# The way out of an RWKV layer: values centred before the recurrence, group norm with tokens on the partitions, the output product one half of the tokens at a time, and experts chosen on the logits

## The chip, the cores and the metric

The kernel runs on one core of a Trainium2 chip. The metric is the device time of one execution in microseconds (us), the median of three. The core's engines run side by side, each through its own list of instructions in order, and wait for each other on semaphores: TensorE (PE), VectorE (DVE), ScalarE (ACT), GpSimd (POOL), and SyncE (SP), which here only issues DMAs. Matrix products land in PSUM, 8 banks of 512 fp32 columns on 128 partitions; everything else lives in SBUF.

## The reference

The kernel computes two decoder layers on 256 tokens of width 1024, with 16 learned tokens ahead. Only the end of the second layer's RWKV part and the start of its experts matter here. Cut to that:

```python
def step(S, inp):                        # per head of 64: matrix state S
    sa = einsum('bhvk,bhk->bhv', S, a_t)
    S = S * w_t + sa[..., None] * b_t + v_t[..., None] * k_t
    return S, einsum('bhvk,bhk->bhv', S, r_t)
_, out = lax.scan(step, S0, xs)
mu  = mean(out, axis=-1)                 # over the 64 values of a head
var = mean(square(out - mu), axis=-1)
out = (out - mu) * rsqrt(var + GN_EPS) * gn_w + gn_b
y = (out + bonus).reshape(B, T, D)
h = h + (y * g) @ w_o
u = rmsnorm(h, ffn_norm)
probs = softmax(u @ w_router)            # 8 experts, top 2, their share renormalised
```

## The kernel before

Each engine's program is written out by hand in the order in which it runs; a `wait_ge(semaphore, n)` holds the engine until another has counted that far. Nothing is scheduled automatically, so an engine's order is the order of the code.

**The recurrence** is done in 5 chunks of 64 positions (`NCH`, the index `c`; the first holds padding and the learned tokens). Tensors stand with channels on the partitions: 8 pairs of heads (`PAIRS`), a pair's two heads on partitions 0 to 63 and 64 to 127 (`HROWS`). First a triangular system is solved for all chunks at once (`level_y` L1045, `level_x` L1060; ACT takes each result out of PSUM at L1581). Then the loop over chunks: right-hand side (L1079, L1082; evicted by ACT L1591), solution U (L1089; evicted by DVE L2068), state update (L1100, L1102; DVE L2073, L2080) and, from chunk 1 on, the outputs (L1112, L1114, L1116; evicted by ACT L1595 into `w_a`, channels on the partitions). The state and the outputs are linear in the values `v_a`, which are turned per chunk and head by a product with a 64x64 unit matrix (`turned`, kind "TV").

**The exit.** After the last chunk PE turns the residual `hT` into token order (L1125, 16 transposes), sums each head's outputs with `headones` (L1130), DVE subtracts the mean (L2089), ACT squares (L1604), PE sums the squares (L1136), ACT takes the root (L1607), and DVE does four operations on each of 8 pairs: reciprocal, gain, bias plus bonus, gate (L2092 to L2099). The output product (L1146) contracts over channels: 8 steps, each for both halves of the tokens (`t`) and both halves of the columns (`n`), so that all four results end together. DVE adds the residual (L2105), ACT squares and roots (L1611, L1613), DVE normalises (L2113), PE turns the normalised tokens (L1158), ACT copies them (L1621) and PE makes the logits (L1166, 16 products of 8 columns). DVE then softmaxes and picks two experts in 20-odd small steps (L2131 to L2150), PE ranks the tokens (L1172 to L1176), and the tokens of the first two experts are gathered (L1190).

**The experts** come last: 8 experts, every one over all its weights, streamed by SP into a ring of 7 tiles of 1 MB, split by ACT and DVE into two fp32r parts (L1640, L2179) and multiplied at L1237 to L1239. Ahead of the logits, ACT and DVE already split the first two tiles (L1617, L2118). SP starts to load this ring when the last outputs are evicted (L488, L485). POOL makes the low half of the normalised tokens (L618) from ACT's high half (L1624).

## Time and profile before

| | us |
|---|---|
| median of three runs | 1696.16 (1696.04 to 1699.24) |
| the profiled execution, its own time | 1698.43 |
| its span, from first to last instruction | 1696.7 |
| PE busy | 1643.3 (97%) |
| DVE busy | 1263.2 (74%) |
| ACT busy | 985.2 (58%) |
| POOL busy | 86.1 (5%) |

The busy share alone says that PE works nearly always. Where it does not, and what it does at the exit of the recurrence, is seen in the views by time. All times in this document that have the form of a place (at 644.5) are microseconds from the start of the span.

### The profile page before, as it was taken

To read this page: it belongs to the slowest core of one execution; us is meant where nothing else is said; L and a number is where in the kernel's file an instruction comes from. 1 tells how busy PE (TensorE), PEld (TensorE's weight loads), DVE (VectorE), ACT (ScalarE), POOL (GpSimd) and SP (SyncE) were. 2 spreads that over 40 slices of the span, in tenths; PEclk is the share of its full clock that TensorE was granted. 3 is DMA by queue.
4 is the path that set the end of the run, shared out by engine and by line. 5 is a ranking of instruction groups with operands and counts; after the bars stand their busy time and mean duration, and the time that the engine had idled before them with its cause. 6 is when DMAs were issued, how large, how long until landed. Compare 5 with 4: busy or idle time off the path is not lost.

```text
span 1696.7 us, 27438 instructions
## 1 busy us (share of the span) xinstructions
PE 1643.3 (97%) x11321; PEld 1405.2 (83%) x11321; DVE 1263.2 (74%) x1202; ACT 985.2 (58%) x1003; POOL 86.1 (5%) x134
## 2 busy tenths in 40 slices
PE   7999999998999999699999999999999999999997
PEld 5879999997778996588888888888888888888885
DVE  4655555534486746598888898988988988898986
ACT  5655443331423222577667776767767777767674
POOL 3462000001000000100000000000000000000000
PEclk9989999999999999799999999999999999999999
DMA  7115555542440005199999999999999999999993
GB/s 276 51 51 186 179 176 178 176 150 58 148 144 6 3 4 187 64 358 380 378 356 343 366 364 372 374 341 357 372 354 384 364 349 353 369 361 381 363 373 148
DMA packets 191312, 432.66 MB, mean 255 GB/s; under 512 B 10003, under 2 KB 11027, under 8 KB 191188
## 3 DMA queue, kind: packets, MB, share of 16 engines
q1 hardware_dynamic: 191148, 430.82, 70.8%
q8 instruction: 91, 1.49, 0.4%
q14 instruction: 33, 0.27, 0.0%
q10 hardware_dynamic: 40, 0.08, 0.0%
HBM read 429.82 MB, written 1.05 MB: 254 GB/s over the span
## 4 chain that ended last, share of the span: by engine, by line
PE 90%; DVE 5%; ACT 3%; issue 1%; DMA 0%; ACTq 0%; DVEq 0%
PE ps L1237 18%; PE ps L1239 18%; PE ps L1238 18%; PE ps L682 6%; PE ps L684 6%; PE ps L683 6%; PE ps L926 3%; PE ps L1146 2%; PE ps L1261 1%; PE ps L1060 1%; PE ps L1045 1%; PE ps L1190 1%; PE ps L1004 1%; DVE arena L1984 1%; PE ps L1016 1%
## 5 line engine op out<-in xcount | busy, mean ns | idle before, releaser
L2179 DVE TENSOR_TENSOR wsplit<-raw_w,wsplit 128x2048 fp32r<-128x2048 f32 x336 | 751.4, 2287 | 78.4 <-ACT wsplit L1640 78.4
L1640 ACT ACTIVATE wsplit<-raw_w 128x2048 fp32r<-128x2048 f32 x336 | 624.9, 1918 | 59.4 <-PE ps L1239 59.4
L1237 PE MATMUL ps<-wsplit,xsplit 128*128 128x512 f32 x896 | 354.4, 396 | 0.0
L1239 PE MATMUL ps<-wsplit,xsplit 128*128 128x512 f32 x896 | 349.7, 390 | 0.0
L1238 PE MATMUL ps<-wsplit,xsplit 128*128 128x512 f32 x896 | 349.1, 390 | 0.0
L1239 PEld LDWEIGHTS ps<-wsplit,xsplit 128*128 128x128 f32 x896 | 168.2, 188 | 35.8
L1237 PEld LDWEIGHTS ps<-wsplit,xsplit 128*128 128x128 f32 x896 | 168.3, 188 | 33.4 <-DVE wsplit L2179 0.5
L1238 PEld LDWEIGHTS ps<-wsplit,xsplit 128*128 128x128 f32 x896 | 168.6, 188 | 33.1
L1237 PE MATMUL ps<-wsplit,hsplit 128*128 128x512 f32 x448 | 175.3, 391 | 1.5 <-DVE hsplit L2209 1.5
L1238 PE MATMUL ps<-wsplit,hsplit 128*128 128x512 f32 x448 | 174.5, 390 | 0.0
L1239 PE MATMUL ps<-wsplit,hsplit 128*128 128x512 f32 x448 | 174.5, 389 | 0.0
L1677 ACT ACTIVATE arena<-ps 128x512 f32<-128x512 f32 x56 | 33.5, 598 | 178.6 <-PE ps L1239 178.6
L1886 DVE TENSOR_TENSOR ffn_lo<-ffn_raw,ffn_hi 128x2048 fp32r<-128x2048 f32 x42 | 95.0, 2293 | 53.4 <-ACT ffn_hi L1480 53.2
L684 PE MATMUL ps<-u_hi,ffn_lo 128*128 128x272 f32 x448 | 129.0, 288 | 0.0
L683 PE MATMUL ps<-u_lo,ffn_hi 128*128 128x272 f32 x448 | 128.9, 288 | 0.0
L682 PE MATMUL ps<-u_hi,ffn_hi 128*128 128x272 f32 x448 | 128.9, 288 | 0.0
L1480 ACT ACTIVATE ffn_hi<-ffn_raw 128x2048 fp32r<-128x2048 f32 x42 | 78.6, 1903 | 37.8 <-PE ps L684 37.8
L1237 PEld LDWEIGHTS ps<-wsplit,hsplit 128*128 128x128 f32 x448 | 84.2, 188 | 18.7 <-DVE wsplit L2179 1.7
L926 PE MATMUL ps<-arena 128*128 128x272 f32 x384 | 93.8, 403 | 5.6 <-DVE arena L1938 5.1
L1239 PEld LDWEIGHTS ps<-wsplit,hsplit 128*128 128x128 f32 x448 | 84.1, 188 | 17.7
L1238 PEld LDWEIGHTS ps<-wsplit,hsplit 128*128 128x128 f32 x448 | 84.2, 188 | 16.9
L926 PEld LDWEIGHTS ps<-arena 128*128 128x128 f32 x384 | 73.5, 194 | 24.4 <-issue 6.4
(395 smaller groups left out, 2324.1 us busy)
## 6 DMA issues: line engine op xcount, KB each, us to landing
raw_w<-in_moe_w_gate SPq DMA_DIRECT2D x114, 1024.0 KB, 7.1
raw_w<-in_moe_w_up SPq DMA_DIRECT2D x112, 1024.0 KB, 7.8
raw_w<-in_moe_w_down SPq DMA_DIRECT2D x112, 1024.0 KB, 7.1
ffn_raw<-in_ffn_w_up SPq DMA_DIRECT2D x14, 1024.0 KB, 5.1
ffn_raw<-in_ffn_w_gate SPq DMA_DIRECT2D x14, 1024.0 KB, 5.2
ffn_raw<-in_ffn_w_down SPq DMA_DIRECT2D x14, 1024.0 KB, 5.1
ffn_raw<-in_attn_w_qkv SPq DMA_DIRECT2D x6, 1024.0 KB, 10.8
ffn_raw<-in_attn_w_o SPq DMA_DIRECT2D x4, 1024.0 KB, 11.0
```

The lines of the kernel that those rows point to most:

```text
L682: mm(o, w_hi_, x_hi_, start=first, stop=False)
L683: mm(o, w_hi_, x_lo_, start=False, stop=False)
L684: return mm(o, w_lo_, x_hi_, start=False, stop=last_)
L926: last = mm(ps[:, j % 4, 0:T], slot_k[s][:, k, (m % 4) * P:(m % 4 + 1) * P], xm[which // 2][:, k, :], start=(k == 0), stop=(k == KC - 1))
L1146: last = mm(ps[:, 2 * t + n, :], w_a[:, k, CH + t * P:CH + (t + 1) * P], slot_k[n][:, k, :], start=(k == 0), stop=(k == KC - 1))
L1237: mm(o, x_[0], w_[0], start=first_, stop=False)
L1238: mm(o, x_[0], w_[1], start=False, stop=False)
L1239: return mm(o, x_[1], w_[0], start=False, stop=last_)
L1480: A(ffn_hi[:, m % NFH, :], ffn_raw[:, ffn_at(m), :], ACT.Copy).then_inc(hi_ok, 1)
L1640: A(wsplit[:, m % NRING, 0, :], raw_w[:, m % NRAW, :], ACT.Copy).then_inc(w_hi, 1)
L1886: v.tensor_tensor(ffn_lo[:, ffn_at(m), :], ffn_raw[:, ffn_at(m), :], ffn_hi[:, m % NFH, :].bitcast(F32), ALU.subtract).then_inc(lo_ok, 1)
L2179: v.tensor_tensor(wsplit[:, m % NRING, 1, :], raw_w[:, m % NRAW, :], wsplit[:, m % NRING, 0, :].bitcast(F32), ALU.subtract).then_inc(w_lo, 1)
```

## The change

**Centring.** The matrix that turns the values is no longer the unit matrix but the unit matrix less 1/64, `wide`, built by POOL. The values, and with them state and outputs, come out less their mean over the head; the mean is never computed from the outputs.

**Outputs by tokens.** The two operands of the output products change places, so that tokens stand on the partitions: chunks 1 and 2 are the first 128 tokens, 3 and 4 the second. A pair's two heads write the same 64 partitions of two banks, 6 and 7, where before each wrote its own 64 partitions of one bank. The outputs stay in PSUM. ACT squares them there (`gn_squares`), DVE sums over each head (`gn_sums`), ACT takes the root of 16 numbers per token (`gn_root`), DVE scales (`gn_scaled`), PE turns them back (`y_turned`), and DVE gates them (`gated`) with two prepared tensors. For the first half all this stands inside the loop, in chunks 2 to 4.

**Prepared tensors.** POOL makes (bonus + bias) * gate and gate * gain ahead, behind `bonus_ok`. The residual is turned into token order much earlier, ahead of the projections, and copied by ACT into `htok`.

**The output product** runs one quarter after the other (`out2(t, n, ...)`). What stands in between: the turning of the second half of the outputs, of the finished tokens (not yet normalised, `tokens_turned`), and the first three quarters of the logits. The gain of the norm is multiplied into the router's weights, and the token's own scale into the logits.

**The choice** works on the logits: softmax is taken out of the way, and the exponentials are used only for the shares of the two chosen.

**Tables.** ACT gets a dummy Sqrt ahead of the loop over chunks and a dummy Exp ahead of the split of the tokens, so that the function tables are loaded there.

```diff
@@ POOL: the centring matrix, behind the masks; the prepared tensors @@
+            fill(wide[:, :], -1.0 / HD)
+            one(g.affine_select(out=wide[:, :], in_=wide[:, :], pattern=[[-1, P]], compare_op=ALU.not_equal, fill=1.0 - 1.0 / HD,
+                                base=0, channel_multiplier=1), masks_ok)
...
-            pool.wait_ge(utT_mm, 4)
+            pool.wait_ge(bonus_ok, 1)
+            pool.wait_ge(l2_ev, 3 * KC)
+            for m in range(PAIRS):
+                last = g.tensor_scalar(bonus[:, m, :], bonus[:, m, :], par[:, m, R_GNB:R_GNB + 1], None, ALU.add)
+            one(last)
+            one(g.tensor_tensor(bonus[:, :, :], bonus[:, :, :], g_a[:, :, :], ALU.mult))
+            for m in range(PAIRS):
+                last = g.tensor_scalar(g_a[:, m, :], g_a[:, m, :], par[:, m, R_GNW:R_GNW + 1], None, ALU.mult)
+            own.done(last, gb_ok)
@@ PE: the residual turned ahead of the projections; the values @@
+            for t in range(2):
+                for half in range(2):
+                    for q in range(4):
+                        k = 4 * half + q
+                        last = tr(ps[:, 4 + 2 * t + half, q * P:(q + 1) * P], hT[:, k, META + t * P:META + (t + 1) * P], ident[:, :])
+                    last.then_inc(ht_mm, 1)
...
-                        unit = mask64[rows, 8, :] if kind == "TV" else Dg[rows, c, p, :]
+                        unit = wide[rows, rows] if kind == "TV" else Dg[rows, c, p, :]
@@ PE: the loop over chunks @@
+            def y_turned(t):
+                pe.wait_ge(yn_ok, t + 1)
+                for h in range(2):
+                    for q in range(4):
+                        last = tr(ps[:, 4 + h, q * P:(q + 1) * P], yn[:, 4 * h + q, :, :].rearrange("p a d -> p (a d)"), ident[:, :])
+                    last.then_inc(yt_mm, 1)
...
+                if c == NCH - 1:
+                    y_turned(0)
                 if c:
+                    t, toks = (c - 1) // 2, HROWS[(c - 1) % 2]
                     for h in range(2):
                         pe.wait_ge(u_ev, c * 2 + h + 1)
-                        if c >= 2:
-                            pe.wait_ge(ot_ev, (c - 2) * 2 + h + 1)
+                        if t:
+                            pe.wait_ge(yn_ok, 1)
                         for p in range(4 * h, 4 * h + 4):
-                            o = [ps[rows, 6 + h, (p % 4) * CH:(p % 4 + 1) * CH] for rows in HROWS]
+                            o = [ps[toks, 6 + e, p * CH:(p + 1) * CH] for e in range(2)]
                             for e, rows in enumerate(HROWS):
-                                mm(o[e], S[(c - 1) % 2][rows, p, :], r_a[rows, p, cs_(c)], start=True, stop=False)
+                                mm(o[e], r_a[rows, p, cs_(c)], S[(c - 1) % 2][rows, p, :], start=True, stop=False)
...
@@ PE: behind the loop, in place of L1120 to L1168 @@
+            out2(0, 0, range(KC))
+            y_turned(1)
+            out2(0, 1, range(KC))
+            out2(1, 0, range(KC))
+            tokens_turned(0, 0)
+            tokens_turned(0, 1)
+            out2(1, 1, range(4))
+            logits(0, 0)
+            logits(0, 1)
+            tokens_turned(1, 0)
+            out2(1, 1, range(4, KC))
+            logits(1, 0)
+            tokens_turned(1, 1)
+            logits(1, 1).then_inc(lg_mm, 1)
@@ ACT @@
+            A(mstat[:, 1, 0:1], epsD, ACT.Sqrt)
             for c in range(NCH):
                 for h in range(2):
                     act.wait_ge(rhs_mm, c * 2 + h + 1)
                     A(RHS[:, 4 * h:4 * h + 4, :], quad(h), ACT.Copy).then_inc(rhs_ev, 1)
...
+                if c == 3:
+                    gn_root(0)
+                if c == 2 or c == 4:
+                    gn_squares(c // 2 - 1)
+            gn_root(1)
...
+            square_tokens(0)
             for m in range(AHEAD):
                 act.wait_ge(ring_in[m], ring_was[m] + 16)
                 A(wsplit[:, m, 0, :], raw_w[:, m, :], ACT.Copy).then_inc(w_hi, 1)
...
+            turned(0)
+            turned(1)
+            turned(2)
+            square_tokens(1)
+            A(mstat[:, 1, 0:1], epsD, ACT.Exp)
             for t in range(2):
+                act.wait_ge(utok_ok, 2 * t + 2)
                 A(utok_hi[:, t, :], utok[:, t, :], ACT.Copy).then_inc(utok_hi_ok, 1)
@@ DVE @@
+                if c == 3:
+                    gn_sums(0)
                 for h in range(2):
                     dve.wait_ge(u_mm, c * 2 + h + 1)
                     v.tensor_copy(U[:, 4 * h:4 * h + 4, :], quad(2 + h)).then_inc(u_ev, 1)
+                if c == 3:
+                    gn_scaled(0)
...
+            gated(0)
+            dve.wait_ge(ld_router, 16)
+            v.tensor_tensor(router[:, :, :], router[:, :, :], par[:, :, R_FFNN + 1:R_FFNN + 2].to_broadcast([P, KC, EXPERTS]), ALU.mult)
+            gn_sums(1)
+            gn_scaled(1)
...
             dve.wait_ge(lg_mm, 1)
-            step(v.tensor_copy(rt(3), ps[:, 0, 0:16].rearrange("p (t e) -> p t e", t=2)))
-            step(v.tensor_reduce(col(0), rt(3), AX, ALU.max))
-            step(v.tensor_tensor(rt(1), rt(3), wide(0), ALU.subtract), lg_sub)
-            dve.wait_ge(lg_exp, 1)
-            step(v.tensor_reduce(col(1), rt(2), AX, ALU.add))
-            step(v.reciprocal(col(2), col(1)))
-            step(v.tensor_tensor(rt(3), rt(2), wide(2), ALU.mult))
+            step(v.tensor_tensor(rt(3), ps[:, 0, 0:16].rearrange("p (t e) -> p t e", t=2), wide(7), ALU.mult))
+            step(v.tensor_reduce(col(3), rt(3), AX, ALU.max))
+            step(v.tensor_tensor(rt(1), rt(3), wide(3), ALU.subtract), lg_sub)
```

How instructions move is shown at three places. First PE from the last outputs of the last chunk on. Before (L1116 outputs, L1125 residual turned, L1130 and L1136 sums over heads, L1146 output product):

```order
L1116 MATMUL ps<-arena 64x64 x2
L1125 MATMUL ps<-ident,hT 128x128 [waits ot_ev]
L1125 MATMUL ps<-ident,hT 128x128 x15
L1130 MATMUL ps<-arena,headones 128x256 x4
L1130 MATMUL ps<-arena,headones 128x256 [waits gn_x] x4
L1136 MATMUL ps<-arena,headones 128x256 [waits gn_sqd,ht_cp]
L1136 MATMUL ps<-arena,headones 128x256 [waits gn_sqd] x3
L1136 MATMUL ps<-arena,headones 128x256 [waits gn_sd,gn_sqd] x4
L1146 MATMUL ps<-arena 128x512 [waits slot_in1,y_ok,slot_in0,gn_sd]
L1146 MATMUL ps<-arena 128x512 x3
```

The same place in the changed kernel (L1147 outputs, L1156 output product, L1097 outputs turned, L1167 tokens turned, L1173 logits):

```order
L1147 MATMUL ps<-arena 64x64 x2
L1156 MATMUL ps<-arena 128x512 [waits y_ok,slot_in1,slot_in0]
L1156 MATMUL ps<-arena 128x512 [waits y_ok] x7
L1097 MATMUL ps<-ident,arena 128x128 [waits yn_ok]
L1097 MATMUL ps<-ident,arena 128x128 x7
L1156 MATMUL ps<-arena 128x512 x8
L1156 MATMUL ps<-arena 128x512 [waits y_ok] x8
L1167 MATMUL ps<-ident,arena 128x128 [waits yn_ok,acc_ok]
L1167 MATMUL ps<-ident,arena 128x128 x3
L1167 MATMUL ps<-ident,arena 128x128 [waits yn_ok,acc_ok]
L1167 MATMUL ps<-ident,arena 128x128 x3
L1156 MATMUL ps<-arena 128x512 x4
```

The output product now stands right behind the outputs, and 8 + 8 transposes and part of the logits stand between its quarters. Second, ACT where the loop over chunks begins. Before (L1581 the triangular system, L1591 right-hand sides, L1595 outputs):

```order
L1581 ACTIVATE arena<-ps 128x512 [waits x_mm] x23
L1591 ACTIVATE arena<-ps 128x256 [waits rhs_mm] x4
L1595 ACTIVATE arena<-ps 128x4x64 [waits ot_mm] x2
L1591 ACTIVATE arena<-ps 128x256 [waits rhs_mm] x2
L1595 ACTIVATE arena<-ps 128x4x64 [waits ot_mm] x2
```

Now (L1628 the dummy Sqrt, L1632 right-hand sides, L1621 squares, L1626 the root):

```order
L1609 ACTIVATE arena<-ps 128x512 [waits x_mm] x23
L1628 ACT_TABLE_LOAD
L1628 ACTIVATE mstat<-normcol 128x1
L1632 ACTIVATE arena<-ps 128x256 [waits rhs_mm] x6
L1621 ACTIVATE arena<-ps 128x512 [waits ot_mm]
L1621 ACTIVATE arena<-ps 128x512
L1632 ACTIVATE arena<-ps 128x256 [waits rhs_mm] x2
L1626 ACTIVATE qstat<-qstat,normcol 128x16 [waits gn_ss]
```

A table load and the dummy stand between the last eviction of the system and the first right-hand side; the evictions of outputs are gone, and two squares stand ahead of chunk 3's right-hand sides. Third, DVE from the third residual sum to the first step of the choice. Before, all four residual sums stood together ahead of the norm (L2105) and the two splits (L2118) right ahead of the choice (L2131). Now (L2180 the splits, L2162 residual sums, L2185 a turned quarter copied, L2166 and L2170 the norm, L2198 and after it the choice):

```order
L2180 TENSOR_TENSOR wsplit<-raw_w,wsplit 128x2048 [waits w_hi] x2
L2162 TENSOR_TENSOR arena<-arena,ps 128x512 [waits wo2_mm] x2
L2185 COPY arena<-ps 128x4x128 [waits utT_mm]
L2166 RECIPROCAL rcol<-rcol 128x1 [waits n4_std]
L2170 SCALAR_TENSOR_TENSOR utok<-arena,rcol 128x512 [waits dve_own]
L2170 SCALAR_TENSOR_TENSOR utok<-arena,rcol 128x512
L2198 TENSOR_TENSOR route<-ps,rcol 128x2x8 [waits lg_mm]
L2199 TENSOR_REDUCE rcol<-route 128x2 [waits dve_own]
L2200 TENSOR_TENSOR route<-route,rcol 128x2x8 [waits dve_own]
```

The splits have moved ahead of the last two residual sums; from the first step of the choice to the mask that PE waits for there are now 14 steps on DVE, with no wait for ACT among them.

## Rows read from the trace of the kernel before

**Rows 1.** Windows: stretch, its length, busy time of the engines, granted clock, DMA share, GB/s

```profile
685.00:714.00 29.00, 16.25 (x91) 14.23 (x92) 17.09 (x42) 14.44 (x23) 4.65 (x2) 0.71 0.21 73
714.00:1000.00 286.00, 286.00 (x1310) 237.24 (x1309) 250.13 (x152) 210.12 (x155) 0.00 (x0) 1.00 0.98 357
```

**Rows 2.** What SP's queue waited for: total us, times, longest

```profile
SPq L485 <- DVE wsplit L2179: 842.8, 329, 24.8
```

**Rows 3.** The chain that ended last, in order of time: start, us, what

```profile
644.48 0.39 ACT arena L1595
644.92 1.97 PE ps L1125 x16
...
656.47 27.72 PE ps L1146 x64
...
684.21 0.70 DVE arena L2105
684.93 1.16 ACT utok L1611 x2
686.11 0.30 ACT rcol L1613
...
690.63 4.59 PE ps L1166 x32
...
701.24 0.59 PE ps L1172 x2
...
713.97 0.23 PE ps L1237
```

**Rows 4.** Timeline of ACT: start, us, instruction, idle time before it and its releaser

```profile
610.84 0.82 ACT L1591 ACTIVATE arena<-ps 128x256 f32<-128x256 f32 x2
...
630.86 0.38 ACT L1595 ACTIVATE arena<-ps 128x256 f32<-128x256 f32 x1 [1.02 <-PE ps L1116]
...
651.27 1.28 ACT L1607 ACT_TABLE_LOAD   x1
...
691.82 2.02 ACT L1624 ACTIVATE utok_hi<-utok 128x1024 fp32r<-128x1024 f32 x2
```

**Rows 5.** Timeline of PE, the outputs of chunk 3

```profile
635.59 0.28 PE L1112 MATMUL ps<-arena 64*64 64x64 f32 x4
635.71 0.28 PE L1114 MATMUL ps<-arena 64*64 64x64 f32 x4
```

**Rows 6.** Timeline of DVE in chunk 3 and in the choice of experts

```profile
633.89 0.42 DVE L2068 COPY arena<-ps 128x256 f32<-128x256 f32 x1 [0.27 <-PE ps L1089]
...
698.92 0.18 DVE L2140 TENSOR_TENSOR route<-route,rcol 128x16 f32<-128x16 f32 x1
...
701.00 0.18 DVE L2146 TENSOR_TENSOR route<-route 128x16 f32<-128x16 f32 x1
```

**Rows 7.** DVE by line and form: a sum over 256 columns

```profile
L1734 DVE TENSOR_REDUCE kstat<-rsq 128x4 f32<-128x256 f32 x2 | 0.8, 414 | 1.7 <-ACT rsq L1359 1.7
```

**Rows 8.** Timeline of PE in the attention of layer 0

```profile
85.00 0.73 PE L728 MATMUL ps<-kz,qT 64*128 64x272 f32 x4
85.56 0.41 PE L731 MATMUL ps<-kz,qT 64*128 64x144 f32 x4
```

**Rows 9.** Timelines of POOL and DVE side by side, early and at the choice

```profile
64.16 4.58 POOL L550 TENSOR_TENSOR ffn_lo<-ffn_raw,ffn_hi 128x2048 fp32r<-128x2048 f32 x1
...
78.00 3.14 POOL L559 TENSOR_SCALAR probs<-probs,stat 128x144 f32<-128x144 f32 x4 [5.78 <-DVE stat L1801]
...
693.07 4.65 POOL L618 TENSOR_TENSOR utok_lo<-utok,utok_hi 128x1024 fp32r<-128x1024 f32 x2 [276.64 <-ACT utok_hi L1624]
...
65.08 3.68 DVE L1799 TENSOR_TENSOR stat<-stat 128x4 f32<-128x4 f32 x1 [2.08 <-ACT stat L1406]
...
695.66 2.09 DVE L2133 TENSOR_TENSOR route<-route,rcol 128x16 f32<-128x16 f32 x1
```

**Rows 10.** Timeline of PE at the start of the projections

```profile
403.61 16.69 PE L926 MATMUL ps<-arena 128*128 128x272 f32 x55 [5.10 <-DVE arena L1938]
```

More of the change, by code:

```diff
@@ L1115, in _ @@
                             for e, rows in enumerate(HROWS):
-                                last = mm(o[e], v_a[rows, p, cs_(c)], both[c][1][rows, 0, p, :], start=False, stop=True)
+                                last = mm(o[e], both[c][1][rows, 0, p, :], v_a[rows, p, cs_(c)], start=False, stop=True)
+                    if c % 2 == 0:
                         last.then_inc(ot_mm, 1)
-            pe.wait_ge(ot_ev, 2 * (NCH - 1))
-            for t in range(2):
-                for half in range(2):
-                    for q in range(4):
-                        k = 4 * half + q
-                        last = tr(ps[:, 2 * t + half, q * P:(q + 1) * P], hT[:, k, META + t * P:META + (t + 1) * P], ident[:, :])
-                    last.then_inc(ht_mm, 1)
@@ L1139, in _, with out2, tokens_turned @@
-            pe.wait_ge(gn_sd, PAIRS)
+            def out2(t, n, ks):
+                for k in ks:
+                    if n == 0:
+                        pe.wait_ge(y_ok, 2 * t + k // 4 + 1)
+                    last = mm(ps[:, 2 * t + n, :], w_a[:, k, CH + t * P:CH + (t + 1) * P], slot_k[n][:, k, :],
+                              start=(k == 0), stop=(k == KC - 1))
+                    if k == KC - 1:
+                        last.then_inc(wo2_mm, 1)
+            def tokens_turned(t, half):
+                pe.wait_ge(acc_ok, 2 * t + half + 1)
+                if t == 0:
+                    pe.wait_ge(yn_ok, 2)
+                for q in range(4):
+                    k = 4 * half + q
+                    last = tr(ps[:, (6, 4)[t] + half, q * P:(q + 1) * P], acc[:, t, k * P:(k + 1) * P], ident[:, :])
+                last.then_inc(utT_mm, 1)
@@ L1509, in _ @@
             norm_std_(3)
+            act.wait_ge(norm_u, KC)
+            act.wait_ge(ht_mm, 4)
+            for n in range(4):
+                own.done(A(htok[:, n // 2, (n % 2) * BLK:(n % 2 + 1) * BLK], ps[:, 4 + n, :], ACT.Copy), ht_cp)
             def take(j):
@@ L1586, in quad, with gn_squares, gn_root @@
                 return ps[:, b, 0:4 * CH].rearrange("p (a b) -> p a b", a=4)
+            def gn_squares(t):
+                act.wait_ge(ot_mm, t + 1)
+                if t:
+                    act.wait_ge(gn_ss, t)
+                for e in range(2):
+                    last = A(gsq[:, e, :, :], ps[:, 6 + e, :].rearrange("p (a b) -> p a b", a=PAIRS), ACT.Square)
+                own.done(last, gn_sqd)
+            def gn_root(t):
+                act.wait_ge(gn_ss, t + 1)
+                own.done(A(qstat[:, 1, t, :], qstat[:, 0, t, :], ACT.Sqrt, bias=eps_gn, scale=1.0 / HD), gn_sd)
+            A(mstat[:, 1, 0:1], epsD, ACT.Sqrt)
             for c in range(NCH):
@@ L1613, in _, with turned @@
                 own.done(A(rcol[:, 6, t:t + 1], normcol[:, 2, t:t + 1], ACT.Sqrt, bias=epsD, scale=1.0 / D), n4_std)
+            def turned(n):
+                t, half = n // 2, n % 2
+                act.wait_ge(utT_mm, n + 1)
+                own.done(A(utT[:, 4 * half:4 * half + 4, t * P:(t + 1) * P],
+                           ps[:, (6, 4)[t] + half, :].rearrange("p (a b) -> p a b", a=4), ACT.Copy), utT_cp)
+            square_tokens(0)
             for m in range(AHEAD):
@@ L2119, in _ @@
                     .then_inc(w_lo, 1)
+            added(2)
+            added(3)
+            dve.wait_ge(utT_mm, 4)
+            own.done(v.tensor_copy(utT[:, 4:8, P:2 * P], ps[:, 5, :].rearrange("p (a b) -> p a b", a=4)), utT_dve)
+            normed(1)
             col = lambda n: rcol[:, n, :]
```

157 lines of the change are left out of this document (62 added, 95 removed).

## The prediction, made before the changed kernel was run

> **What bounds the kernel now.** I read the windows first. From 714 to 1000 PE is busy in all of 286.00 us [rows 1], and so on to the end of the experts, at the full granted clock. The weights come at 357 GB/s and the DMA share is 0.98, which could make the stream the bound; but SP's queue spent 842.8 us, in 329 waits, on DVE's freeing of a ring tile [rows 2]: it waits for buffers, not they for it. So the experts last as long as PE needs, whenever they start, and what counts is when the first expert product (L1237) starts: at 713.97 [rows 3]. In the window 685 to 714 PE is busy in 16.25 of 29.00 us at a mean clock of 0.71 [rows 1].
>
> The chain in order of time then gives the exit piece by piece [rows 3]. The last outputs are evicted from 644.48. The output product starts at 656.47: 12.0 us for residual, sums over heads and norm. It takes 27.72 us for 64 records, two for each of the 32 products, so 0.87 us for each. The last residual sum is at 684.21, the logits start at 690.63, and PE's ranks wait until 701.24. From the end of the product to the ranks it is 17.0 us, and from the ranks to L1237 12.7 us, which the change leaves alone.
>
> **The change part by part.** Terms are shifts of L1237, plus is later.
>
> *Ahead of the loop over chunks.* The dummy Sqrt makes a table load of 1.28 us, which stood at 651.27 in the exit, stand ahead of ACT's first right-hand sides at 610.84 [rows 4]. PE has nothing to do there but the solution that needs them, and the whole loop is a chain behind it. With 0.3 for the dummy itself: **+1.6**. The Trainium skill (ScalarE: Activation LUTs, What ACT_TABLE_LOAD costs) puts a switch of sets at about 2.66 us, the load and a drain as long again. The trace has the load at 1.28 us and the next operation of ACT right behind it. By the page the term would be +2.9.
>
> *In the loop.* The output products keep count and shape; a pair's products follow each other every 0.12 us [rows 5], 24 pairs a chunk in four chunks. They now share the 64 output columns of the array and lie on different rows of it. The trace has that form in attention: L728 is two products of 64 rows on the same 128 output partitions, two banks, 272 columns, in 4 records. One such record takes 0.23 us (0.433 for 512 columns [rows 3], by 272/512). Four in a row would be 0.92; L731 starts 0.56 behind L728 [rows 8]. So they overlap; I take 0, bounds 0 and +11.2 (96 pairs at 0.117).
>
> Group norm of the first half: ACT squares from 630.86, where it evicted outputs before [rows 4], two PSUM operations, about 1.1; chunk 3's right-hand sides are queued behind them on ACT, wanted at 631.8 and so late by 0.1 with as much cover. DVE sums 1024 columns: 0.41 for 256 [rows 7] with about 0.17 of fixed cost (a step on 16 columns takes 0.18 [rows 6]) makes 1.2, done at 633.2, just when U can be copied. ACT's root hides behind the copies, the second of which is at 633.89 to 634.3 [rows 6]; reciprocal and two scalings (0.7 and 0.6, by the 0.70 of L2105 [rows 3]) end at 635.95. PE wants banks 6 and 7 for chunk 3 at 635.59 [rows 5] and now waits for that, with the outputs and all of chunk 4 queued behind: **+0.4**. The state update behind the scalings is late by 1.2, with 2 us of cover while the outputs run. If the squares came an operation later, this wait would grow one for one.
>
> The turn of the first half in chunk 4 is 8 of the 16 transposes that took 1.97 [rows 3]: **+1.0**. DVE's gating of it (4 operations of 0.7) ends before the last outputs do.
>
> *Behind the loop.* The product starts right behind the outputs instead of 12.0 us after 644.48: **-12.0**. Its 27.7 us stay. In between stand 8 transposes for the second half, 12 for finished tokens and 8 of 16 logit products: 20 x 0.123 + 8 x 0.287 (4.59 for 16 [rows 3]) = 2.5 + 2.3: **+4.8**. The waits in between are covered: the second half's norm needs about 4.5 us behind the last outputs, the first quarter gives 6.9; its gating is done within 4 us under the second quarter; DVE's two weight splits, 4.5 us, lie under the third.
>
> *From the end of the product to the ranks*, 17.0 before. Now: residual sum 0.15 + 0.7, square and root 1.5 (684.93 to 686.41 [rows 3]) with 0.1 ahead, so the root at +2.5. DVE normalises till +4.2; the last logits, on PE, are ready at +3.9. Then 14 steps to the mask, 0.208 apart (ten intervals from 698.92 to 701.00 [rows 6]), 2.9: the mask at +7.1, if nothing holds DVE. But ACT behind its root loads Exp (1.3, dummy 0.2) and copies the first half of the tokens (1.0, half of 2.02 [rows 4]); so POOL starts on the low half at about +5.2, when DVE stands at its sixth or seventh step, and works 2 x 2.33 us. A DVE operation on two SBUF operands doesn't run beside a two-operand one of POOL: one on 4 columns took 3.68 us and ended with POOL's from 64.16 to 68.74, and in the choice itself one took 2.09 us, till POOL ended at 697.72 [rows 9]. Most of the 14 steps are of that kind. So they end with POOL at +9.9, and six or seven more steps, 1.4, make +11.3: **-5.7**. Half of what removing steps saves is given back there.
>
> *At no cost.* The 16 early transposes stand in a gap of PE: it idles 5.10 us until 403.61 [rows 10]; at 0.123 they need 2.0, at half clock 4.0. ACT's four copies fall into its own gap there. If they ran over, the projections would start that much later. POOL's preparation starts at about 538 and needs, at 0.79 for each of 16 (3.14 for 4 [rows 9]) and 4.6 for the product, some 18 to 20 us; it is wanted at 642. It can hold DVE's two-operand steps in the grouping (up to 4.6 once); PE there runs eight banks ahead, over 6 us, so 0, bounds 0 and +4.6. The ring starts to fill some 3 us later, and the first tile is wanted 16 us after that.
>
> Sum: 1.6 + 0.4 + 1.0 - 12.0 + 4.8 - 5.7 = -9.9. The profiled execution is 1698.43 with a span of 1696.7, 2.3 above the median of 1696.16; the shift is the same for both. 1698.4 - 9.9 = 1688.5 for a profiled one, and **1686.3** as the median.
>
> **The rivals.**
> *The array doesn't overlap two products that share output columns.* Then each of 96 pairs costs 0.117 more, +11.2; and if the start-up seen in attention (0.56 against 0.46 for two records) is paid by every pair, another 0.1 each, +9.6. 1686.3 + 11.2 to + 20.8 is 1697.5 to 1707: slower. It decides from 0.10 us a pair. For it: no row has this form with 64 columns on 64. Against it: the attention products, as worked out above [rows 8]. The Trainium skill (TensorEngine Tiling (Array Packing), Gotcha 1: PSUM Pressure) says that different row tiles can't access one bank at the same time and go to different ones; banks 6 and 7 keep to that, so by the page too they overlap.
>
> *POOL doesn't hold DVE in the choice* (its start falls later, or DVE slips through). The mask is then at +7.1: -9.9 for that term, and 1682.1. For it: only a few tenths between the seventh step and POOL's start. Against it: DVE would need to finish seven more steps in that time.
>
> *The moved work delays the loop*: norm in chunk 3 late by one or two operations, POOL's preparation felt by PE, +2 to +5, so 1688 to 1691. For it: the chain squares, sums, root, reciprocal, scalings crosses engines five times, and I have 0.4 of its end uncovered.
>
> *The gain doesn't reach the end* since the stream sets the pace of the experts: the ring would be full either way at the start, so the time is before's plus what the ring fills later, 1696 to 1699. Against it: PE has no gap there, and the queue waits for buffers [rows 1, 2].
>
> **How the numbers follow.** Forecast 0.64; POOL doesn't hold 0.12; the loop delayed 0.14; gain lost in the stream 0.04; no overlap 0.06. The range must leave out no more than 2 in 10: from 1681.5 (POOL doesn't hold) to 1691.2 (the far end of loop delayed). 0.2% of this time, 3.4 us, is about what a measurement of this kernel can tell from no change; the border is at 1692.8. Faster: the first three, less a little of the delayed one for worse than I bound it, 0.88. Same: the stream and the mild end of no overlap, 0.07. Slower: the rest, 0.05.
>
> **What the profile of the changed kernel would show.** A table load between the last L1609 and the first L1632 of ACT, and the first solution (L1117) 1.6 us later behind the system than now. The outputs' pairs still 0.12 apart. A wait of PE for DVE's scalings ahead of chunk 3's outputs, below a microsecond. The output product right behind the outputs, and no wait of over 0.5 us until the logits are done. One or two DVE steps of over a microsecond in the choice, beside POOL. L1237's successor starting at about 704, and the experts as long as now (983 us from there to the span's end). The prediction is wrong if the pairs lie 0.23 apart, if PE waits for norm or gating between the quarters, or if the experts are longer.

## The result, and the profile after

The changed kernel took 1684.63 us (median; 1682.65 to 1686.13) against 1697.32 for the kernel before, measured beside it: a ratio of 0.9925, 95% interval 0.9913 to 0.9936. Two later measurements of the same pair gave 0.9949 (0.9935 to 0.9962) and 0.9919 (0.9905 to 0.9932), so 12.7, 8.5 and 13.5 us less. The mean of the three ratios, 0.9931, times 1696.16 is 1684.5; 1686.3 was predicted.

The chain that ended last, in order of time, of the changed kernel (start, us, what) stands against [rows 3]:

```profile
645.90 7.06 PE ps L1156 x16
652.97 0.87 PE ps L1097 x8
653.84 13.73 PE ps L1156 x32
667.57 0.88 PE ps L1167 x8
668.45 3.43 PE ps L1156 x8
671.88 1.69 PE ps L1173 x16
673.57 0.49 PE ps L1167 x4
674.06 3.45 PE ps L1156 x8
677.53 0.70 DVE arena L2162
678.25 1.16 ACT utok L1641 x2
...
682.53 2.13 DVE route L2207
684.68 2.27 DVE route L2209
...
688.25 0.60 PE ps L1196 x2
...
693.94 6.15 PE ps L1214 x24
...
701.66 0.23 PE ps L1261
```

The four quarters of the output product (L1156) follow each other, with turns and logits between them and no wait. They take 27.67 us together, as the product did before (27.72). Then comes the choice, with two steps above 2 us, and the first expert product (L1261) at 701.66 instead of 713.97 [rows 3]. One wait of PE stands outside this chain, ahead of the last quarter of the logits. The timeline of PE has it:

```profile
679.72 1.06 PE L1173 MATMUL ps<-router,arena 128*128 128x8 f32 x8 [0.78 <-DVE arena L2185]
```

The front of the kernel, nearly the same in both, doesn't take the same time in each execution. A timeline of ScalarE shows where the front ends, at the last result of the triangular system (L1609, before L1581). Changed kernel:

```profile
609.38 0.60 ACT L1609 ACTIVATE arena<-ps 128x512 f32<-128x512 f32 x1 [0.34 <-PE ps L1080]
609.99 1.28 ACT L1628 ACT_TABLE_LOAD   x1
611.29 0.20 ACT L1628 ACTIVATE mstat<-normcol 128x1 f32<-128x1 f32 x1
611.40 0.64 ACT L1632 ACTIVATE arena<-ps 128x256 f32<-128x256 f32 x2
```

and the kernel before:

```profile
610.35 0.60 ACT L1581 ACTIVATE arena<-ps 128x512 f32<-128x512 f32 x1 [0.34 <-PE ps L1060]
```

In the profiles of this study that place lies anywhere from 605.84 to 612.00. So below, kernels are compared by the **stretch** from there to the first expert product in the timeline of PE: 713.81 - 610.35 = 103.46 before, 701.49 - 609.38 = 92.11 after. From that product to the span's end it is 982.9 us in both. The gain of the change is thus 11.35 us in the first profile of the changed kernel, and 11.6 and 11.5 in its two repeats, each against the one profile of the kernel before.

### The profile page after: what moved, and what is told of

It is laid out like the page before. It is cut to its first block, busy times and chain, and to the rows that moved or that the text cites. A ratio compares the mean times of both kernels' runs of the same rounds, so it can differ in the third digit from the quotient of the medians.

```text
span 1684.4 us, 27376 instructions
## 1 busy us (share of the span) xinstructions
PE 1631.8 (97%) x11305; PEld 1396.5 (83%) x11305; DVE 1250.3 (74%) x1176; ACT 977.8 (58%) x986; POOL 107.9 (6%) x153
## 4 chain that ended last, share of the span: by engine, by line
PE 89%; DVE 6%; ACT 3%; issue 1%; DMA 0%; ACTq 0%; DVEq 0%
PE ps L1261 18%; PE ps L1263 18%; PE ps L1262 18%; PE ps L694 6%; PE ps L696 6%; PE ps L695 6%; PE ps L944 3%; PE ps L1156 2%; PE ps L1285 1%; PE ps L1065 1%; PE ps L1080 1%; PE ps L1214 1%; PE ps L1024 1%; DVE arena L2022 1%; PE ps L1036 1%
## 5 line engine op out<-in xcount | busy, mean ns | idle before, releaser
L1261 PE MATMUL ps<-wsplit,xsplit 128*128 128x512 f32 x896 | 354.3, 395 | 0.0
L1261 PEld LDWEIGHTS ps<-wsplit,xsplit 128*128 128x128 f32 x896 | 168.3, 188 | 33.3 <-DVE wsplit L2244 0.5
L1261 PE MATMUL ps<-wsplit,hsplit 128*128 128x512 f32 x448 | 175.2, 391 | 1.5 <-DVE hsplit L2274 1.5
L1261 PEld LDWEIGHTS ps<-wsplit,hsplit 128*128 128x128 f32 x448 | 84.1, 188 | 18.7 <-DVE wsplit L2244 1.7
```

The costliest lines, as they stand in the source:

```text
L1261: mm(o, x_[0], w_[0], start=first_, stop=False)
```

## The experiments

Each row is one kernel. The first two numbers are its median and that of the kernel before, measured beside it; the last three are read from one profile of it. "Below" and "above" in what follows compare stretches with those of the three profiles of the changed kernel, unless medians are named.

| kernel | median, before beside it | ratio (95%) | front ends | first expert product | stretch |
|---|---|---|---|---|---|
| before | | | 610.35 | 713.81 | 103.46 |
| changed | 1684.63, 1697.32 | 0.9925 (0.9913-0.9936) | 609.38 | 701.49 | 92.11 |
| changed again | 1687.64, 1696.18 | 0.9949 (0.9935-0.9962) | 610.67 | 702.52 | 91.85 |
| changed, third time | 1683.89, 1697.42 | 0.9919 (0.9905-0.9932) | 608.10 | 700.10 | 92.00 |
| load later | 1683.01, 1696.18 | 0.9928 (0.9914-0.9941) | 605.84 | 696.39 | 90.55 |
| heads apart | 1694.13, 1696.18 | 0.9982 (0.9973-0.9991) | 610.15 | 712.00 | 101.85 |
| not quartered | 1692.47, 1697.42 | 0.9971 (0.9959-0.9982) | 605.98 | 704.38 | 98.40 |
| choice alone (on before) | 1695.80, 1697.42 | 0.9993 (0.9984-1.0002) | 610.45 | 713.33 | 102.88 |
| low early | 1683.59, 1697.42 | 0.9912 (0.9897-0.9927) | 610.70 | 700.36 | 89.66 |
| low split | 1681.33, 1696.18 | 0.9907 (0.9892-0.9922) | 612.00 | 699.53 | 87.53 |
| clock held | 1685.41, 1697.42 | 0.9926 (0.9911-0.9941) | 610.70 | 700.75 | 90.05 |
| two edits | 1680.03, 1697.42 | 0.9899 (0.9883-0.9915) | 610.03 | 696.49 | 86.46 |
| two edits again | 1679.22, 1697.42 | 0.9889 (0.9874-0.9905) | 609.12 | 695.25 | 86.13 |
| three edits | 1676.39, 1697.42 | 0.9877 (0.9860-0.9894) | 607.73 | 691.51 | 83.78 |

**The changed kernel twice more.**

> The changed kernel once more, as it is, so that the edits of this group can be compared with it on the same chip. Expected: the ratio to the kernel before of the first measurement again, 0.9925, so 12 to 13 us less. One thing is open in its first profile: the front of the kernel, which the change does not touch, reached the norm ahead of the projections 2.6 us earlier than in the profile of before (396.52 against 399.13), with a granted clock of 1.00 against 0.89 in the window 60 to 140. If that belongs to the execution and not to the change, the place varies among the profiles of these runs, which all have the same front.

> The changed kernel a third time. The two measurements so far gave 0.9925 and 0.9949 of the kernel before, whose intervals don't meet, while the stretch from the triangular system's last result to the first expert product was 92.0 and 91.7 us in the two profiles, against 103.3 in the kernel before. Theory (the gain is 11.3 to 11.6 us, a ratio of 0.9932, and the rest is how the front of the kernel happens to run): the stretch is again 91.5 to 92.2, and the ratio between the two.

The stretch repeats within 0.3 us, the place where the front ends does not. Window 60 to 140 (its length, busy time of PE, PEld, DVE, ACT, POOL, granted clock, DMA share, GB/s) of the kernel before:

```profile
60.00:140.00 80.00, 75.00 (x504) 65.55 (x503) 48.16 (x151) 50.45 (x138) 54.04 (x85) 0.89 0.23 80
```

of the changed kernel, first profile:

```profile
60.00:140.00 80.00, 72.05 (x532) 62.98 (x531) 51.46 (x157) 53.37 (x147) 56.33 (x90) 1.00 0.24 83
```

and of the changed kernel, second profile:

```profile
60.00:140.00 80.00, 75.02 (x505) 65.23 (x502) 47.97 (x151) 50.71 (x140) 53.79 (x85) 0.89 0.23 80
```

The clock of 1.00 belonged to the execution, not to the change: the repeat has 0.89 like the kernel before, and its front ends at 610.67 against 610.35. The clock in that window isn't all of it: the third profile has 0.98 there and its front ends earliest of the three, at 608.10. What else moves the front wasn't tried.

**The table load later.**

```diff
-            A(mstat[:, 1, 0:1], epsD, ACT.Sqrt)
             for c in range(NCH):
                 for h in range(2):
...
+                if c == 0:
+                    A(mstat[:, 1, 0:1], epsD, ACT.Sqrt)
```

> One edit on the changed kernel: the dummy Sqrt that brings the table load stands behind chunk 0's right-hand sides on ScalarE instead of ahead of them; ScalarE idles there for over 3 us. Theory (the load stood on the path, 1.28 for the load and 0.2 for the dummy): the first solution and all behind it come 1.5 us earlier, and the time is 1.5 us below that of the changed kernel. Rival (the solution waits for something else that ends as late, for instance the last result of the triangular system): the load is hidden either way, and the time is the same. The page's price, load and drain (the Trainium skill, ScalarE: Activation LUTs), would give up to 2.9 us.

Stretch 90.55, 1.3 to 1.6 below the three of the changed kernel. ScalarE's timeline of this kernel:

```profile
605.84 0.60 ACT L1609 ACTIVATE arena<-ps 128x512 f32<-128x512 f32 x1 [0.34 <-PE ps L1080]
606.33 0.38 ACT L1631 ACTIVATE arena<-ps 128x256 f32<-128x256 f32 x1
607.11 0.38 ACT L1631 ACTIVATE arena<-ps 128x256 f32<-128x256 f32 x1 [0.40 <-PE ps L1107]
607.51 1.28 ACT L1633 ACT_TABLE_LOAD   x1
```

The first right-hand side now starts 0.49 behind the system's last result; it was 2.02. So the load and its dummy stood on the path at 1.5 us. The Trainium skill (ScalarE: Activation LUTs, What ACT_TABLE_LOAD costs) has 2.66 us for load and drain. Taking load and dummy away gave back 1.3 to 1.6, so the measurement decides here. The median is 4.6 below that of the changed kernel measured beside it, three times what the stretch gives; the front of its profile ends 4.8 earlier.

**Heads apart.** In each half of the pairs the products of one head of every pair, then those of the other:

```diff
-                        for p in range(4 * h, 4 * h + 4):
-                            o = [ps[toks, 6 + e, p * CH:(p + 1) * CH] for e in range(2)]
-                            for e, rows in enumerate(HROWS):
-                                mm(o[e], r_a[rows, p, cs_(c)], S[(c - 1) % 2][rows, p, :], start=True, stop=False)
...
+                        for e, rows in enumerate(HROWS):
+                            for p in range(4 * h, 4 * h + 4):
+                                o = ps[toks, 6 + e, p * CH:(p + 1) * CH]
+                                mm(o, r_a[rows, p, cs_(c)], S[(c - 1) % 2][rows, p, :], start=True, stop=False)
...
```

> On the changed kernel: the same output products, but not in pairs. For each half of the pairs all 12 products of the heads on partitions 0 to 63 are issued first, then the 12 of the heads on 64 to 127, so neighbours use the same 64 rows of the array and can't run side by side. Theory (the changed kernel's pairs do overlap while sharing the 64 output columns): 96 pairs lose their overlap, each costs 0.117 us more, and the time is 11 us above the changed kernel, less what lay in waits of TensorE (under 1 us). Rival (they don't overlap in the changed kernel, and the pitch of 0.117 for a pair is what two such products need one after the other): the time is that of the changed kernel.

Stretch 101.85, 9.7 to 10.0 above. Not all of that is the edit's. In this profile the granted clock was 0.50 from 614.4 to 617.6, ahead of the first output product (622.37), and the first copy of U in chunk 1 came 6.57 behind the first of chunk 0 where the changed kernel has 5.03. Less these 1.5 the edit cost 8.2 to 8.5 us instead of the 11 expected, 0.09 for each of 96 pairs; the medians differ by 6.5. Timeline of PE, changed kernel, a pair (4 records, two for each product) in each row:

```profile
645.27 0.28 PE L1147 MATMUL ps<-arena 64*64 64x64 f32 x4
645.38 0.28 PE L1143 MATMUL ps<-arena 64*64 64x64 f32 x4
```

and with heads apart, one product (2 records) in each row:

```profile
656.18 0.28 PE L1143 MATMUL ps<-arena 64*64 64x64 f32 x2
656.30 0.28 PE L1144 MATMUL ps<-arena 64*64 64x64 f32 x2
```

In both kernels the rows follow each other every 0.117 us in the mean, but a row of the first holds two products and one of the second a single one. So pairs that share 64 output columns, on different rows and in different banks, do run side by side. Without the overlap the loss was 8.2 to 8.5 us where the first rival was priced at 11.2 and more; where one head's group of products ends and the other's begins, some still overlapped.

**Not quartered.** The product runs over all four quarters, channel by channel, behind the norm of the second half; the turned tokens, the logits and all four residual sums stand behind it:

```diff
-            out2(0, 0, range(KC))
             y_turned(1)
-            out2(0, 1, range(KC))
...
+            for k in range(KC):
+                pe.wait_ge(y_ok, 3 + k // 4)
+                for t in range(2):
+                    for n in range(2):
+                        last = mm(ps[:, 2 * t + n, :], w_a[:, k, CH + t * P:CH + (t + 1) * P], slot_k[n][:, k, :],
...
```

> On the changed kernel, the division into quarters alone is undone: TensorE turns back the second half of the outputs as soon as they are normalised, then runs the output product over all four quarters together, channel by channel as the kernel before did, and turns the tokens and makes all logits behind it. Centring, outputs by tokens, the norm of the first half inside the loop and the choice on the logits stay. Places are counted from the last result of the triangular system, since the front of the kernel varies by some microseconds from one profile to the next. Theory (the quarters hide the norm of the second half, and the residual sums, squares and turns of the first): the product starts about 6.7 us behind the outputs instead of 0.1, nothing stands inside it (3.9 us less), and from its end to the choice it takes 2.3 us longer: about 5 us above the changed kernel. Rival A (the quarters are worth nothing, the norm would be over early enough): the same time. Rival B (nearly all of the gain is theirs, and the move of the norm into the loop brings nothing): 10 us or more above.

Stretch 98.40, 6.3 to 6.6 above, between theory and rival B. Its timeline of PE around the norm:

```profile
646.94 1.84 PE L1097 MATMUL ps<-ident,arena 128*128 128x128 f32 x8 [4.48 <-DVE arena L2115]
649.50 2.93 PE L1184 MATMUL ps<-arena 128*128 128x512 f32 x3 [0.73 <-DVE arena L2128]
```

and its windows:

```profile
649.50:653.00 3.50, 3.50 (x4) 1.51 (x5) 2.40 (x3) 2.36 (x2) 0.00 (x0) 0.50 1.05 390
```

PE waited 4.48 us for the scalings, turned in 1.84 what takes 1.04 in the timeline of the changed kernel, and ran the first products at 0.50 of the clock. The whole product took 29.89 us in the chain instead of 27.67. These 2.2 us are what the estimate had left out: a second price of the stall, since PE came back at half clock. In the kernel before, PE had waited 1.12 and 1.32 us ahead of the product with work between, was granted 1.00, and the product took 27.72: there that price wasn't paid. So undoing the quarters costs 6.3 to 6.6 of the 11.5 us. The rest, some 5.0 if the parts add, is left for the centring, the outputs by tokens, the norm inside the loop and the choice; the next run doesn't give the share of the choice, and no run takes the others apart.

**The choice alone**, on the kernel before:

```diff
-            dve.wait_ge(lg_exp, 1)
-            step(v.tensor_reduce(col(1), rt(2), AX, ALU.add))
-            step(v.reciprocal(col(2), col(1)))
-            step(v.tensor_tensor(rt(3), rt(2), wide(2), ALU.mult))
...
```

> On the kernel before, one part of the change alone: the two experts are chosen on the logits, and the exponentials are used for the shares only; the four steps that made probabilities ahead of the choice go. Theory (VectorE stands behind GpSimd until 697.7 in the profile of before whatever the steps are, and 11 steps of 0.21 us follow where 16 did): the mask 1.1 us earlier, and the time 1.1 us below the kernel before, a ratio of 0.9993. Rival (the whole of the removed steps and of the wait for the exponential counts): 1.9 us below. Neither can be told from no change by the times; the place of the mask in the profile tells it.

The mask comes 700.19 - 610.45 = 89.74 behind the front's end, against 701.00 - 610.35 = 90.65: 0.9 earlier where 1.1 was expected. But the way there is not the one of the theory. Timelines of this profile:

```profile
690.47 6.97 PE L1166 MATMUL ps<-router,arena 128*128 128x8 f32 x32 [1.26 <-ACT arena L1621]
...
692.91 4.64 POOL L618 TENSOR_TENSOR utok_lo<-utok,utok_hi 128x1024 fp32r<-128x1024 f32 x2 [275.99 <-ACT utok_hi L1624]
...
697.48 0.17 DVE L2131 COPY route<-ps 128x16 f32<-128x16 f32 x1 [4.90 <-PE ps L1166]
```

The logits took 6.97 us instead of 4.58: in the window 690 to 695 PE was granted 0.50 here and 0.83 in the profile of the kernel before. So the choice started 2.2 later than there, at 697.48, when GpSimd was all but done, and none of its steps was held. The mask followed 2.71 behind the first step, where it took 5.75 before. That the 0.9 is near the 1.1 is luck: the profile doesn't show that GpSimd absorbs what the removed steps save, nor what they save when the logits are in time. The stretch is 0.6 shorter, and the ratio can't be told from 1.

**GpSimd's low half.** In the changed kernel, timelines of ScalarE, GpSimd and VectorE:

```profile
681.15 1.99 ACT L1662 ACTIVATE utok_hi<-utok 128x1024 fp32r<-128x1024 f32 x2
682.27 4.64 POOL L630 TENSOR_TENSOR utok_lo<-utok,utok_hi 128x1024 fp32r<-128x1024 f32 x2 [125.90 <-ACT utok_hi L1662]
682.33 0.17 DVE L2206 TENSOR_REDUCE rcol<-route 128x2 f32<-128x16 f32 x1
682.53 2.12 DVE L2207 TENSOR_TENSOR route<-expno,rcol 128x16 f32<-128x16 f32 x1
684.68 2.26 DVE L2209 SCALAR_TENSOR_TENSOR route<-route 128x16 f32<-128x16 f32 x1
```

Here is the edit of "low split". "Low early" has it without the last two lines, GpSimd's wait for the ranks. In both the buffers of `utok_hi` and of an expert's results are exchanged:

```diff
+            def high_tokens(t):
+                act.wait_ge(utok_ok, 2 * t + 2)
+                A(utok_hi[:, t, :], utok[:, t, :], ACT.Copy).then_inc(utok_hi_ok, 1)
...
             turned(1)
+            high_tokens(0)
             turned(2)
             square_tokens(1)
             A(mstat[:, 1, 0:1], epsD, ACT.Exp)
...
+            high_tokens(1)
...
                 pool.wait_ge(utok_hi_ok, t + 1)
+                if t:
+                    pool.wait_ge(rank_mm, 1)
```

> On the changed kernel, the first half of the edit that split GpSimd's low half: the first 128 tokens are made early, the second at once when ScalarE has their high half, as in the changed kernel. Theory (each 2.33 us piece of GpSimd holds VectorE once): one step above 1 us is left in the choice, and the stretch from the triangular system to the first expert product is 2.1 us below the changed kernel. Rival (one piece is as bad as two, because the step that it meets waits for the whole of it and the order of steps moves with it): within 1 us of the changed kernel.

> On the changed kernel: ScalarE makes the high half of the first 128 tokens right behind the copies of those tokens, at about 673 instead of 681, so GpSimd does its low half while VectorE has nothing to do; and GpSimd waits with the low half of the second 128 tokens until TensorE has done the ranks. (The buffer of the high halves changes places with that of an expert's results, which is needed for the earlier copy and moves nothing else.) Theory (GpSimd's 4.64 us hold VectorE's steps of 2.12 and 2.26 us in the choice): both long steps become 0.18, the mask and the ranks come 4.0 us earlier, and the second low half (2.3 us from the ranks) ends before the first gather wants it (3.4 us behind the ranks). Time 4.0 us below the changed kernel. Rival (the long steps have another cause, or the first gather then waits for the low half): the steps stay above 1 us, or the gather waits, and the time is less than 1.5 us below.

Low early: stretch 89.66, 2.2 to 2.5 below, one long step left. Low split: 87.53, 4.3 to 4.6 below, where 4.0 was expected; the gathers make up some of it (7.02 us from the first to the first expert product, 7.34 to 7.55 in the changed kernel). Their timelines of DVE, low early first:

```profile
684.02 2.20 DVE L2212 SCALAR_TENSOR_TENSOR route<-route 128x16 f32<-128x16 f32 x1
```

```profile
685.12 0.18 DVE L2212 TENSOR_TENSOR route<-expno,rcol 128x16 f32<-128x16 f32 x1
685.34 0.17 DVE L2214 SCALAR_TENSOR_TENSOR route<-route 128x16 f32<-128x16 f32 x1
```

That settles the cause of the long steps: each half of GpSimd's work that meets the choice holds VectorE once, for what is left of that half.

**The clock held.** Seven products behind the logits and three behind the ranks, whose results nobody reads, keep PE at work:

```diff
+            def idle_products(n):
+                for _ in range(n):
+                    mm(ps[:, 7, :], ident[:, :], acc[:, 0, 0:BLK], start=True, stop=True)
+            idle_products(7)
...
+            idle_products(3)
```

> On the changed kernel: while TensorE waits for the choice it does products that nobody reads (seven of 512 columns behind the logits, three behind the ranks, 0.87 us each at the full clock), so that it is not idle from 681 to 688. Theory (the granted clock of 0.50 from 684 to 698 in the profile comes from that idleness and costs time): the granted clock stays 1.00, the ranks take 1.2 us instead of 2.25, the gathers come 0.8 us apart instead of 0.98, and the first expert product comes 2 to 2.5 us earlier behind the mask. Rival A (the gathers are held by the copies of ScalarE and VectorE): under 1.2 us. Rival B (the idle products themselves end later than the mask or the selection and stand in the way): no gain or a loss.

Stretch 90.05, 1.8 to 2.1 below, a little less than expected. The windows of the changed kernel, then of this one:

```profile
684.00:688.00 4.00, 0.00 (x0) 0.00 (x0) 3.78 (x7) 0.00 (x0) 2.91 (x2) 0.50 0.00 0
688.00:690.50 2.50, 2.25 (x10) 2.21 (x10) 0.86 (x5) 0.00 (x0) 0.00 (x0) 0.50 0.00 0
...
694.00:698.00 4.00, 4.00 (x17) 3.70 (x17) 0.76 (x2) 1.32 (x4) 0.00 (x0) 0.50 0.00 0
```

```profile
686.00:690.00 4.00, 2.62 (x10) 1.07 (x9) 3.69 (x10) 0.00 (x0) 2.21 (x1) 1.00 0.00 0
690.00:694.00 4.00, 4.00 (x13) 1.98 (x13) 1.74 (x9) 1.28 (x1) 0.00 (x0) 0.62 0.00 0
```

The ranks ran at full clock, but then it fell all the same after 1.4 us without work, and the three products behind the ranks, at half clock, ended late: DVE had made the selection at 694.16, and the first gather started at 694.63, behind them.

**Together.**

> The changed kernel with two edits together: the table load behind chunk 0's right-hand sides, and the low half of the first 128 tokens made early, of the second behind the ranks. In the profiles of the single edits they shortened the way from the triangular system to the first expert product by 1.5 and 4.3 us. They lie at different places of one chain, so they should add: 5.8 us below the changed kernel on the same chip, a ratio to the kernel before of about 0.990. If they don't add, one of them only moved a wait.

> The kernel with two edits once more, so that the third edit can be compared with it on the same chip. Expected: a stretch of 86.3 us from the triangular system to the first expert product, as before, and a time 5.5 us below the changed kernel's.

> The kernel with the two edits that added up (table load behind chunk 0's right-hand sides; GpSimd's low half split) and products that nobody reads while TensorE waits: four of 512 columns behind the logits, three behind the ranks, so that they end ahead of the mask and of the selection. Theory (TensorE at the full granted clock for ranks and gathers saves 1.8 us, as in the profile of the changed kernel with such products, or more, since there the three behind the ranks ran at half clock and ended 0.5 us late): 2 us below the kernel with two edits, a stretch of 84.3 us. Rival (the products end late and eat it up): the same as the kernel with two edits, 86.3.

Two edits: 86.46 and 86.13, 5.4 to 6.0 below; they add. With the third, 83.78: another 2.4 to 2.7. In this last kernel PE makes ranks and gathers at full clock; its windows from 678 to 694 are all at 1.00. The first of the ranks:

```profile
681.02 0.39 PE L1204 MATMUL ps<-route,before 128*128 128x8 f32 x2
```

This version takes 1676.39 us, 21 less than the kernel before and, measured beside it, 7.5 less than the changed one.

## Why the prediction was right

The stretch shrank by 11.35 to 11.6 where 9.9 were predicted: the mechanisms were as described, and the sum came out 1.5 to 1.7 short. By the steps of the prediction, from the rows of the first profile (last system result, first solution L1117 at 611.90 and L1089 at 611.36, last copy of U at 641.98 and 641.64, start of the product in the timelines of PE at 645.83 and 656.47, the rest in the chain):

| step | predicted | measured |
|---|---|---|
| system to first solution | +1.6 | 1.01 to 2.52: +1.5 |
| first solution to last copy of U | +0.4 | 30.28 to 30.08: -0.2 |
| to the output product | +1.0 - 12.0 | 14.83 to 3.85: -11.0 |
| product to last residual sum | +4.8 | 27.74 to 31.70: +4.0 |
| last residual sum to ranks | -5.7 | 17.03 to 10.72: -6.3 |
| ranks to first expert product | 0 | 12.57 to 13.24: +0.7 |
| sum | -9.9 | -11.35 |

- **Right, and tested:** the load's price, 1.5 for 1.6 (load later), the overlap of the pairs (heads apart), POOL holding DVE in the choice (low early, low split). What the quarters are worth was tested as well, but their 6.5 are spread over several terms of the sum. The time followed the stretch, since the experts last 982.9 us in both kernels: the gain wasn't lost in the stream.
- **The loop.** The wait for the scalings was there, at 0.19 instead of 0.4. The loop as a whole was 0.2 shorter: in chunk 1 of the kernel before, the second right-hand side came 1.50 behind the first (615.75, 617.25), in the changed one 0.93 (616.25, 617.18). In the kernel before PE stood still for 0.33 us in that chunk, from 615.97, and the profile names nothing that it waited for. The cause was not looked for by a run.
- **Mis-sized: the logits between the quarters.** They were priced at 0.287 for each of 8 by a stretch of the kernel before [rows 3] of which the window 690 to 695 was granted 0.83 of the clock. At full clock all 8 take 1.69, 0.21 each, and the turns 0.11: 4.0 instead of 4.8.
- **Mis-sized: from the sum to the ranks.** The mechanism is as described, POOL starting 4.7 behind the last residual sum and ending at +9.4. Everything up to there was some 0.4 earlier than summed. 0.15 of it is the step from the end of the product to the residual sum, which was added on the side of the changed kernel alone and is 0.02 in both chains.
- **Missed: the gathers.** "Which the change leaves alone" failed. In the kernel before their products were back at full clock 3.5 us behind the first (706.92), in the changed kernel 6.3 behind it (693.94). From the first gather product to the first expert product it is 7.55 us (7.34 and 7.49 in the repeats) instead of 6.89, and that is the 0.7; holding the clock gave 1.8 to 2.7. Why the clock came back later than in the kernel before is not shown. As a term put at nothing it hid part of what the others were short by. Timelines of PE, before and changed, the first gather product at full clock:

```profile
710.40 0.40 PE L1190 MATMUL ps<-sel,utok_lo 128*128 128x256 f32 x2
```

```profile
700.20 0.40 PE L1214 MATMUL ps<-sel,utok_lo 128*128 128x256 f32 x2
```

- **One sign failed.** "No wait of over 0.5 us until the logits are done": PE waited 0.78 for DVE's copy ahead of the last quarter of the logits. The logits were done at 680.78, DVE's norm at 681.38, so nothing was lost by it.
- **At no cost, as said:** the preparation held VectorE once, for 3.95 us instead of 0.7 (GpSimd's product at 544.20, 4.53 us), and no wait of PE followed. The front of the repeat at the same clock ended 0.3 behind that of before, and the early turns are in it.

```profile
544.20 4.53 POOL L623 TENSOR_TENSOR arena<-arena 128x2048 f32<-128x2048 f32 x1
```

```profile
545.33 3.95 DVE L2079 TENSOR_TENSOR arena<-arena,mask 128x512 f32<-128x512 f32 x1
```

This is what the Trainium skill says (SBUF — State Buffer, Who interferes with whom): an operation of VectorE with two inputs in SBUF and one of GpSimd that reads SBUF exclude each other for a whole instruction. The 2.12, 2.26 and 3.95 us agree. GpSimd's operations with one tensor as input hardly do, though they read SBUF too: beside eight of them VectorE's steps with two inputs took 0.74 and 0.68, and 0.89 once beside eight others.

```profile
548.83 7.54 POOL L625 TENSOR_SCALAR arena<-arena,par 128x256 f32<-128x256 f32 x8
```

```profile
551.24 0.74 DVE L2076 TENSOR_TENSOR arena<-arena,mask 128x512 f32<-128x512 f32 x1
553.10 0.68 DVE L2079 TENSOR_TENSOR arena<-arena,mask 128x512 f32<-128x512 f32 x1
```

What stays open is why the whole-kernel ratios spread (0.9919 to 0.9949) more than their intervals. The front, which ended at 609.38, 610.67 and 608.10 in the three profiles of the changed kernel, spreads as much; what sets it was not found. The medians of the edits spread in the same way: load later has gained 4.6 by its median and 1.5 by its stretch, heads apart has lost 6.5 and 9.7 to 10.0.

## What to carry to other kernels

A stall in front of a long product can be paid twice: here once in a wait of 4.48 us and once more in 2.2 us at half clock behind it. Splitting the product, so that the next part is prepared while the last one runs, removed both. When steps are taken out of a serial stretch, look at what still holds an end there: here GpSimd's low half of the tokens, and only moving that work freed the steps. And where a part common to both kernels spreads by as much as the change is worth, compare the stretch that the change touches and not the span alone. Look at the granted clock inside that stretch too: in two of the profiles here it fell at a place of its own, which cost 1.5 us (heads apart) and 2.4 us (the logits of the choice alone).

## What the runs showed of the hardware

- Products on different rows of the array that write the same 64 columns in two banks overlap fully: 0.117 us a pair, against 0.117 for one alone.
- In the kernel with the clock held, the granted clock still fell behind 6.25 us of uninterrupted products, 1.4 us without work and ranks of 8 columns; in the kernel with three edits, whose ranks came right behind the products, it stayed at 1.00.
- A table load of 1.28 us and a dummy of 0.2 cost 1.3 to 1.6 us on the path, with the next operation directly behind.
- Behind a wait of 4.48 us PE was granted 0.50 until past 653, and 64 records of the output product took 29.89 us; behind waits of 1.12 and 1.32 it was granted 1.00, and they took 27.72.
- VectorE's steps with two inputs in SBUF took 2.12, 2.26 and 3.95 us beside GpSimd's products of two tensors, and 0.74 and 0.68 beside its operations on one.
